# Keys and compressed blocks of the last mixer made inside the feed-forward stage ahead of it, and its second half of heads scored between the first units of attention

## The reference, cut to what matters

```python
def _compress(x_raw, pos, w1, b1, w2):        # 15 blocks of 32 tokens, every 16 tokens
    blocks = x_raw[:, :, idx] + pos
    flat = blocks.reshape(blocks.shape[:3] + (CMP_BLOCK * HEAD_DIM,))
    return jax.nn.gelu(flat @ w1 + b1) @ w2   # flat: 60 rows of 2048; w1: 2048 x 256

def _shared_kv(h, ...):
    kv = (_rmsnorm(h, kv_norm) @ kv_w)        # 6 slots x 4 groups x 64
    k_cmp = _rmsnorm(_compress(kv[0], ...), k_norm[0])
    v_cmp = _compress(kv[1], ...)
    k_sel, k_win = _rmsnorm(kv[2], k_norm[1]), _rmsnorm(kv[4], k_norm[2])
    ...
# layer: h = h + 0.5 * swiglu(...)   (ffn4, 11 blocks of 256 hidden columns)
#        h = h + _nsa(rmsnorm(h), ..., k_cmp, v_cmp, k_sel, v_sel, k_win, v_win)
def _nsa(x, w_qg, q_norm, w_o, ...):
    proj = x @ w_qg                           # 16 heads x 64, and 48 gates
    q = _rmsnorm(q, q_norm); gate = sigmoid(...)
    # per head: softmax over 15 compressed blocks, over selected, over window keys
    out = gate0 * o_cmp + gate1 * o_sel + gate2 * o_win
    return out @ w_o
```

## Time and profile before

| what | value |
|---|---|
| median of 3 runs | 1685.84 us (1684.49 to 1687.93) |
| the profiled execution's own time | 1684.73 us |
| its span, first to last instruction | 1682.9 us |
| PE busy | 1653.2 us, 98% of the span |
| DVE busy, ACT busy | 1020.8 us (61%), 790.9 us (47%) |
| mean granted clock of PE | 0.995 of 2.4 GHz |

### The profile page before, as it was taken

The page is one execution under the profiler, slowest core; times in us unless marked ns, Lnnn a source line. Parts: engine busy times, 40 slices in busy tenths (PEclk is TensorE's granted clock), DMA queues, the critical chain, the costliest instruction groups (busy, mean ns, idle before and its releaser), DMA issues.

```text
span 1682.9 us, 22634 instructions
## 1 busy us (share of the span) xinstructions
PE 1653.2 (98%) x9525; PEld 1424.3 (85%) x9525; DVE 1020.8 (61%) x1067; ACT 790.9 (47%) x954; POOL 60.3 (4%) x73
## 2 busy tenths in 40 slices
PE   8999999999999999999999999999999999899999
PEld 6998888889888887888899888888888886688887
DVE  5776655575465566556676556565555686755555
ACT  5333544454454445444543444445445435744443
POOL 0122000000000001000000000000000030000000
PEclk9999999999999999999999999999999998999999
DMA  7633567655355554665565555557565543045562
GB/s 241 198 109 120 189 198 209 209 189 170 125 188 189 186 200 152 202 211 174 189 212 175 187 175 193 183 182 230 183 207 179 168 143 142 1 138 189 174 208 91
DMA packets 221111, 294.82 MB, mean 175 GB/s; under 512 B 7517, under 2 KB 184881, under 8 KB 221011
## 3 DMA queue, kind: packets, MB, share of 16 engines
q1 hardware_dynamic: 215546, 284.40, 51.0%
q10 hardware_dynamic: 5464, 9.00, 2.1%
HBM read 290.75 MB, written 1.57 MB: 174 GB/s over the span
## 4 chain that ended last, share of the span: by engine, by line
PE 85%; DVE 8%; ACT 4%; issue 2%; DMA 0%; POOL 0%; SPq 0%; ACTq 0%; DVEq 0%; POOLq 0%
PE ps L1834 24%; PE ps L1949 18%; PE ps L1836 12%; DVE wlo L1203 3%; PE ps L1822 3%; PE ps L1825 3%; PE ps L1823 3%; PE ps L1851 3%; PE ps L1857 3%; PE ps L1852 3%; ACT whi L668 2%; PE ps L2045 2%; PE ps L1901 1%; PE ps L1902 1%; PE ps L1903 1%
## 5 line engine op out<-in xcount | busy, mean ns | idle before, releaser
L1203 DVE TENSOR_TENSOR wlo<-raw,whi 128x2048 fp32r<-128x2048 f32 (+2 forms) x270 | 601.3, 2247 | 300.1 <-ACT whi L668 298.9
L668 ACT ACTIVATE whi<-raw 128x2048 fp32r<-128x2048 f32 (+1 forms) x265 | 497.9, 1899 | 66.8 <-PE ps L1825 17.9
L1834 PE MATMUL ps<-x_both,whi 128*128 128x512 f32 x1920 | 480.3, 392 | 0.0
L1834 PEld LDWEIGHTS ps<-x_both,whi 128*128 128x128 f32 x1920 | 348.6, 189 | 64.7
L1836 PEld LDWEIGHTS ps<-x_both,wlo 128*128 128x128 f32 x1920 | 261.9, 190 | 18.7
L1836 PE MATMUL ps<-x_both,wlo 128*128 128x256 f32 x1920 | 267.7, 282 | 0.0
L1949 PE MATMUL ps<-whi,hhi 128*128 128x512 f32 x480 | 187.6, 391 | 0.0
L1949 PE MATMUL ps<-wlo,hhi 128*128 128x512 f32 x480 | 187.5, 391 | 0.0
L1949 PE MATMUL ps<-whi,hlo 128*128 128x512 f32 x480 | 186.7, 389 | 0.0
L750 ACT ACTIVATE hid<-ps 128x512 f32<-128x512 f32 x54 | 32.3, 598 | 225.3 <-PE ps L1836 225.3
L1822 PE MATMUL ps<-x_both,whi 128*128 128x256 f32 x512 | 127.8, 288 | 2.9 <-DVE arena L1363 2.9
(11 more groups left out here) (245 smaller groups left out, 1707.6 us busy)
## 6 DMA issues: line engine op xcount, KB each, us to landing
raw<-in_ffn_w_gate_up SPq DMA_DIRECT2D x80, 1024.0 KB, 5.4
raw<-in_ffn_w SPq DMA_DIRECT2D x62, 1024.0 KB, 5.2
raw<-in_ffn_w_down SPq DMA_DIRECT2D x44, 1024.0 KB, 4.8
raw<-in_hgrn_w_in SPq DMA_DIRECT2D x16, 1024.0 KB, 5.4
raw<-in_moba_w_in SPq DMA_DIRECT2D x12, 1024.0 KB, 5.1
raw<-in_conv_w_in SPq DMA_DIRECT2D x10, 1024.0 KB, 5.6
raw<-in_ffn_w_gate_up SPq DMA_DIRECT2D x16, 512.0 KB, 5.0
raw<-in_kv_w SPq DMA_DIRECT2D x6, 1024.0 KB, 5.1
```

The costliest lines, as they stand in the source:

```text
L668: act.activation(whi[s % WRING][:, 0:width], raw[n % RING][:, 0:width], ACT.Copy).then_inc(split_hi, 1)
L1203: ins = dve.tensor_tensor(wlo[s % WRING][:, part], raw[n % RING][:, part], whi[s % WRING][:, part].bitcast(F32), ALU.subtract)
L1834: pe.matmul(ps[:, bank + n, :], hi[:, k, tile], x_both[:, k], start=k == 0, stop=k == KT - 1, skip_group_check=True)
```

## The change

The keys' normalisation and transposes, the sum of positions and the compression go from `nsa` into the steps of `ffn4`. In steps 3 and 4 of `ffn4` PE transposes keys ahead of its down product, into the two banks that the up product takes next. In steps 5 to 8 it multiplies one `w1` chunk there. The four `w1` chunks are loaded between the chunks of `ffn4`, so they stand in the ring of three with them. DVE and ACT do their parts behind the hidden block of the step and ahead of the split of u(i+1). In `nsa` the first eight heads are scored against the compressed keys as soon as their queries are there, the other eight between the units of the attention. The matmuls on zeros of `nsa` are gone. The key gain takes the factor 1/8 of the logits with it, so the row maxima need no scaling (line 1497 is left out in `nsa`). Two chunks of the output weights are split ahead of the attention, where three were.

The diff, cut to its core (PE, then DVE, then ACT, then the lists of chunks):

```diff
@@ Chunks.plan, and SP's ffn in the same way @@
                 for i in range(2, PAIRS):
                     self.add(name, "g", i)
+                    if name == "ffn4" and i - 1 in COMPRESS:        # COMPRESS = (5, 6, 7, 8)
+                        self.add("nsa", "w1", COMPRESS.index(i - 1), direct=True)
                     if i < PAIRS - 1:
                         self.add(name, "d", i - 1)
                     self.add(name, "u", i)
@@ PE @@
+            def keys_beside(i):
+                if i in (3, 4):
+                    pe.wait_ge(kd_ready, i - 2)
+                    for n in range(2):
+                        for g in range(NG):
+                            mm = pe.transpose(ps[:, 6 + n, g * P:(g + 1) * P], kd[...], ident)
+                        mm.then_inc(kt_turned, 1)
+                if i in COMPRESS:
+                    compress(*divmod(COMPRESS.index(i), 2))        # 16 products of 60 columns
...
                     pe.wait_ge(hlo_ready, hids + i + 1)
+                    if name == "ffn4":
+                        keys_beside(i)
                     down(0, i)
                     used(down(1, i), name, "d", i)
                     if i >= 1:
+                        if name == "ffn4" and i in (3, 4):
+                            pe.wait_ge(kt_kept, 2 * (i - 2))
+                        if name == "ffn4" and i in COMPRESS:
+                            pe.wait_ge(cz_kept, COMPRESS.index(i) + 1)
                         across_pair(6, name, "u", i + 1)
...
             def nsa(name):
                 along(0, 0, name, "first", between=lambda: turn(name, 1))
+                pe.wait_ge(gelu_ready, 1)
+                ...  # 2 products with w2: the compressed keys
                 along(1, 1, name, "first")
                 ...  # gates
-                along(2, 0, name, "q")
+                pe.wait_ge(kd_ready, 3)
+                pe.transpose(ps[:, 7, 0:c], kd[0:c, 16]...).then_inc(kct_turned, 1)
+                along(2, 0, name, "q", between=first_turns)         # turn_q(0), turn_q(1)
                 ...  # gates turned
+                pe.wait_ge(nq_ready, 2)
+                pe.wait_ge(kct_ready, 2)
+                cmp_scores(0)
                 along(3, 1, name, "q")
-                ...  # key transposes, compress x4, turn_q x4, scores of 16 heads, values
-                keep_warm(WARM_CMP, bank=2)                         # 16
-                ...  # transposes of the compressed probabilities, 16 heads
+                pe.wait_ge(gates_ready, 1)
+                pe.wait_ge(cmp_probs, 1)
+                ...  # transposes of the compressed probabilities, 8 heads
@@ PE, attention @@
                 score(0)
-                for i in range(units + 2):
+                score(1)
+                second()          # values of the blocks, turn_q(2), turn_q(3)
+                for i in range(1, units + 2):
+                    beside(i)     # i == 2: waits nq_ready 4 and pt_ready, then cmp_scores(1)
                     if i + 1 < units:
                         score(i + 1)
-                    if i == 0:
-                        keep_warm(warm[0])                          # 12
@@ DVE @@
+            def keys_beside(i):   # behind low_part(i), ahead of split(u, i + 1)
+                if i == 1: ...    # gains, two memsets, mean_square of 16 key columns
+                if i == 2: ...    # scale by krs, duplicate(1)
+                if i == 3: ...    # duplicate(2), positions(0)
+                if i == 4: ...    # positions(1)
+                if i == 5:
+                    compressed(0, 0)      # waits chunk_used of the w1 chunk, adds the bias
+                if i == 6:
+                    compressed(0, 1)
+                    gelu_argument(0)
+                if i == 7: ...    # compressed(1, 0)
+                if i == 8: ...    # compressed(1, 1), gelu_argument(1), end of the keys' gelu
@@ DVE, maxima @@
-                if bias is None:
-                    link(ins)
-                    ins = dve.tensor_scalar(nmax[:, b, :], nmax[:, b, :], scale, None, ALU.mult)
@@ ACT @@
+            def keys_beside(i):   # behind high_part(i), ahead of split(u, i + 1)
+                if i in (3, 4):
+                    for n in range(2):
+                        act.wait_ge(kt_turned, 2 * (i - 3) + n + 1)
+                        act.activation(kt[...], by_k(ps[:, 6 + n, :], NG), ACT.Copy).then_inc(kt_kept, 1)
+                if i == 7:
+                    gelu_sigmoid(0)
```

More of the change, by code:

```diff
@@ L56 @@
 WARM_FINAL = 12
[L57 to L61, removed]
 BY_BLOCK = 6
@@ L570, in ffn @@
                     load(columns(up, i * CW), name, "g", i)
+                    if name == "ffn4" and i - 1 in COMPRESS:
+                        n = COMPRESS.index(i - 1)
+                        load(w["cmp_w1_2"][n // 2, n % 2 * D:(n % 2 + 1) * D, :].rearrange("(k p) n -> p k n", p=P), "nsa", "w1", n)
                     if i < PAIRS - 1:
@@ L1075, in nsa @@
                 act.activation(gates_t[:], ps[0:TAIL, 4, 0:S], ACT.Sigmoid).then_inc(gates_t_ready, 1)
+                act.wait_ge(kct_turned, 1)
+                act.wait_ge(kct_zeroed, 1)
+                for side in range(2):
+                    half = slice(side * HD, (side + 1) * HD)
+                    act.activation(kct[half, :, side, :], by_k(ps[half, 7, 0:NG * N_CMP], NG), ACT.Copy).then_inc(kct_ready, 1)
+                keep_q(0)
+                keep_q(1)
                 act.wait_ge(gates_turned, 1)
@@ new lines, in positions, with compressed @@
+            def positions(a):
+                for half in range(2):
+                    pos = cols[:, R_POS + 16 * a + 8 * half:R_POS + 16 * a + 8 * half + 8].unsqueeze(2).unsqueeze(3)
+                    dve.tensor_tensor(blk[a][:, 8 * half:8 * half + 8, :].rearrange("p j (g n) -> p j g n", g=NG), windows(a, half),
+                                      pos.broadcast_to([P, 8, NG, N_CMP]), ALU.add).then_inc(blocks_ready, 1)
+            def compressed(a, half):
+                dve.wait_ge(chunk_used, chunks.number["nsa", "w1", 2 * a + half] + 1)
+                for n in range(2):
+                    part = slice((2 * a + n) * NG * N_CMP, (2 * a + n + 1) * NG * N_CMP)
+                    b1 = cols[:, R_B1 + 2 * a + n:R_B1 + 2 * a + n + 1] if half == 0 else cz[:, part]
+                    if half == 0:
+                        ins = dve.tensor_scalar(cz[:, part], ps[:, 6 + n, 0:NG * N_CMP], b1, None, ALU.add)
+                    else:
+                        ins = dve.tensor_tensor(cz[:, part], ps[:, 6 + n, 0:NG * N_CMP], b1, ALU.add)
+                ins.then_inc(cz_kept, 1)
+                dve.wait_ge(cz_kept, 2 * a + half + 1)
@@ L1727, in nsa @@
+                split(name, "gates", 0, width=KT * TAIL)
+                dve.wait_ge(gelu_sig, 2)
                 for k in range(2):
@@ new lines, in nsa @@
+                q_scale(1)
+                q_squares(2)
+                cmp_logits(0)
+                cmp_shift(0)
+                q_scale(2)
+                split(name, "out", 0)
+                cmp_scale(0)
+                split(name, "out", 1)
+                q_squares(3)
+                attention(NH // 2, 2, nsa_out,
+                          lambda u: gates[:].rearrange("p t (h b) -> p t h b", b=3)[:, :, 2 * (u // 2):2 * (u // 2) + 2, 1 + u % 2], beside)
+                split(name, "out", 2)
@@ L2368, in nsa @@
                 pe.wait_ge(zero_ready, 4)
-                attention(NH // 2, 2, q_of, k_of, pv, warm=WARM_NSA)
+                pe.wait_ge(q_kept, 4)
+                attention(NH // 2, 2, q_of, k_of, pv, second, beside)
                 out_product(name, pieces=8)
```

433 lines of the change are left out of this document (231 added, 202 removed).

## The result

The changed kernel takes 1692.69 us (median of 9 runs, 1688.83 to 1696.66) against 1685.84 (9 runs): a ratio of 1.0039, 95% interval 1.0027 to 1.0052. The forecast was 1684.4, within 0.2% of no change, with a range up to 1691. The time lies 8.3 us above the forecast and 1.7 above the range. The profiled executions have spans of 1689.4 and 1682.9 us.

What follows compares the result with a forecast made beforehand. The prediction took PE, busy 98% of the span, as the bound. ffn4 22.9 us longer, nsa's head 27.8 sooner and attention 3.5 longer made 1.4 us faster, a median of 1684.4 us, range 1676 to 1691.

Steps and rivals of the forecast that it cites:

- The sum: Whole kernel: ffn4 22.9 us longer, head of nsa 27.8 sooner, attention 3.5 longer, so 1.4 us faster.
- clock 1.00 throughout: Sign expected in the profile after: PE's granted clock stays at its full level, with no slow time.
- rival (a): PE's clock falls behind the second gap in nsa's head: 5 us lost, kernel 3.6 us slower, 1689.4; chance 0.18.
- the first gap: Head of nsa, t0 of the second query half: PE waits 2.5 us for the split of the second q chunk.
- the second gap: Head of nsa, line 1793: PE waits 2.5 us for the scaled compressed probabilities.
- The other row: Window from 448 us: PE idle 0.85 us and clock 0.70, read as a gap followed by the 1.2 GHz level.
- The landing: ffn4, load of g(i+2): 4.9 us from issue to landing, out of 4.8 to 5.5 seen.
- rival (b): Landing in ffn4 takes 6.0 us, deciding from 5.9: ffn4 28.5 us longer, kernel 4.2 slower, 1690.0; chance 0.10.
- The head's waits: Head of nsa: PE waits 2.5 us, 2.5, 1.4 for query quarter 3 and 0.85 for the copy of values.
- The table load: ACT, head of nsa: 1.3 us taken; the skill's 1.38 us of draining on top was left out.
- (c): Rival: the ring's lag is smaller; without 6.6 us of waits in ffn4, 8 us faster, 1677.8; chance 0.22.
- (d): Rival: all waits hide and PE's work alone counts; 18.4 us faster, 1667.4; chance 0.06.

Runs made afterwards that it cites:

- e2: The changed kernel with matmuls on zeros filling PE's gaps in six places, all waits kept; 6.0 us faster than the changed kernel.
- e3: The changed kernel with the four w1 chunks landing in a free stretch of the arena, not the ring of three; 10.8 us faster than the changed kernel.
- e8: The kernel before, with 8 matmuls on zeros in its 2.2 us gap ahead of the compressed-key scores and 28 for 16 behind; ratio 1.0002.
- e9: The changed kernel with matmuls on zeros only ahead of the compressed probabilities and at the start of attention; median 1689.64 us.
- e4: The changed kernel with DVE's order at the head of nsa altered, second q chunk split before the query scalings; median 2.1 us faster than the changed kernel.

## Why the prediction was wrong, step by step

**The step that failed** is the price of PE's clock. The sum puts slow time at nothing ("clock 1.00 throughout"), and only rival (a) prices it: 1.7 us behind the first gap, inside the forecast, and 5 us behind the second, which was to decide. Behind the second gap the profiled execution shows a clock of 1.00, up to the first transposes at 1421.15, so the sign that the prediction names for this case did not come. Four falls elsewhere did. The two behind the last down product and behind the first gap (3.25 us) made the head 3.1 us longer, the one at the start of attention, behind gaps of 0.77, 0.59 and 0.99 us within 5 us, made attention 3.2 longer, and the one in `ffn4` cost 0.9. Together they are 7.2 us by stretches and 6.0 by medians (e2) of the 8.3 missed. With the falls filled up (e2) the head is 28.0 us shorter than before (27.8 forecast) and attention 3.2 us longer (3.5). Unfilled they are 24.9 and 6.4.

One row that spoke against (a) was chance. The gap of 2.88 us near 40 us stands, as long, in all 13 profiled executions, in a part that no edit touches, and in 9 of them the 1.2 GHz level followed. This is e3's:

```profile
40.50 0.58 PE L1912 MATMUL ps<-x_both,whi 128*128 128x256 f32 x1 [2.88 <-DVE arena L1479]
...
40.00:42.00 2.00, 1.50 (x7) 1.50 (x8) 1.65 (x2) 1.25 (x2) 0.00 (x0) 0.52 1.01 389
```

The other row was misread: at 448 us PE is idle not for 0.85 us, which is only what falls into the window, but for 2.43, up to 448.85.

**The landing** was mis-sized. I took 4.9 us for g "since it is alone at the head of the queue", against its own row of 5.5. SP's timeline has the load issued at 1291.72, and ACT's split started at 1297.11, 5.39 us later. Behind it d queues after w1, and once waited 0.51 us in e2. `ffn4` with the clock held is 24.7 us longer, 22.9 forecast; with half the w1 bytes it is 23.5. This is 1.8 us of the miss, and 1.2 of them go with half of w1's bytes. By e3 the moved work is 16.05 us where 16.3 was said, and the waits at full clock 8.6 where 6.6 were walked. The landing may not be all of it, or the walk is long elsewhere: between its own 22.9 (4.9) and 26.0 (5.5) it would have given some 25.4 for 5.39, an estimate, and 24.7 came. It is rival (b) in a mild form: its deciding point of 5.9 us was not reached.

```profile
1291.72 0.37 SPq L528 DMA_DIRECT2D raw<-in_ffn_w_gate_up  x1
```

**The head's waits** were right in kind, and their sum is in part luck. That for the second q chunk was 3.25 instead of 2.5, as POOL's root took 3.56 us where 2.04 was taken, and DVE's scaling of quarter 0 waited 1.08 us for it. That for the compressed probabilities was 1.60 instead of 2.5, quarter 3's 0.77 instead of 1.4. Together the three are 5.6 us, where 6.4 were forecast: one 0.75 too short in the walk, two 0.9 and 0.6 too long.

**The table load** at the head of `nsa` cost what its row shows, and no draining beside it: ACT's split of the gates starts at 1381.87 and takes 0.53 us, and the load starts 0.02 us after it.

```profile
1381.87 0.53 ACT L672 ACTIVATE whi<-raw 128x384 fp32r<-128x384 f32 x1
1382.42 1.28 ACT L742 ACT_TABLE_LOAD   x1
```

**Rivals (c) and (d)**, less or no waiting, did not happen. e3 shows what they would have been worth.

## What to carry to other kernels

Before PE's work is moved into a full stage, ask whose buffer it borrows: a chunk that PE reads directly holds its ring buffer until PE is there, a split chunk only until DVE is, and that difference alone made this change slower instead of faster. A walk of waits on a tuned PE has to price each gap twice, once as idle time and once as slow time that may follow it. One profile in which nothing followed doesn't make a gap safe. The cheap test is to fill the gaps with work that nothing needs. Slow time costs where PE comes last, so a low granted clock in a window is not yet a gain to be had (e8).

## What the runs showed of the hardware

Where the clock falls differs between executions of the same program. The gap of 3.25 us for the second q chunk was followed by the 1.2 GHz level in the changed kernel and not in e9, whose gap there was 3.24:

```profile
1394.00:1400.00 6.00, 5.59 (x32) 4.56 (x32) 0.95 (x2) 1.59 (x4) 1.76 (x1) 1.00 0.52 175
```

In e8 the clock fell at 1404 us, behind 32 small matmuls (128x30) and with no gap of PE above 0.4 us in the 5 us ahead; in e4 at 1405.5, behind 16 of them and a gap of 0.2 (one of 1.46 us lies 8 us back). So idle time is not the only thing that comes ahead of a fall. What brings such a fall on, these runs don't say.

The falls also explain much of the spread between runs (7.8 us for the changed kernel, 4.8 for the kernel before). No edit touches the program ahead of `ffn4`, and still `ffn4`'s first cut lies between 1174.33 and 1179.03 us. Ahead of it the clock fell once in the executions that reach it by 1175.8, twice in those at 1176.2 to 1176.6, three times in those at 1177.4 to 1178.8, and four times in the last: some 1.3 us for each fall. So a difference of 1 or 2 us between medians of 4 to 12 runs is not yet the price of an edit.

A root of 8 columns on POOL took 3.56 and 3.55 us when it began beside a split of DVE, and 1.64 when it did not. Timeline of POOL, changed kernel (DVE's splits run from 1388.36 to 1390.65 and from 1394.32 to 1396.60):

```profile
1388.60 3.56 POOL L1186 TENSOR_TENSOR qrs<-qss,const 128x8 f32<-128x8 f32 x1 [0.67 <-DVE qss L1298]
1394.55 3.55 POOL L1186 TENSOR_TENSOR qrs<-qss,const 128x8 f32<-128x8 f32 x1 [2.40 <-DVE qss L1298]
1405.94 1.64 POOL L1186 TENSOR_TENSOR qrs<-qss,const 128x8 f32<-128x8 f32 x1 [7.84 <-DVE qss L1298]
```

The difference, 1.9 us, is what was left of the split when the root began, 2.05 and 2.05, within 0.2. The 2.04 of the earlier trace rows, which the prediction took, fits the same sum: that root began beside a DVE product of 0.69 us (line 1681) of which 0.54 was left. The Trainium skill ("SBUF — State Buffer", Who interferes with whom) says that "A DVE instruction with two SBUF inputs contends with a GpSimd instruction that reads SBUF"; the split has two, and the trace agrees. So DVE should not have a split right behind the squares whose root is wanted soon, since the root then starts beside it. No kernel here tried that order alone.
